# Moving the column sums one chunk on, the spread behind two rounds, and the output weights' split into the q/k/v stage

## The chip, the cores and the metric

The kernel runs on one core of a Trainium2 chip. The metric is the device time of one execution in microseconds. Engines are named as in the profile: PE is TensorE (PEld its weight loads), DVE is VectorE, ACT is ScalarE, POOL is GpSimd and SP is SyncE, which here only issues transfers. Each engine works through its own list of instructions in order and waits on semaphores that other engines and transfers raise.

## The reference, cut to what matters

Two layers run over 2048 rows of width 1024. Layer 0 is sliding-window attention (16 query heads, 4 key and value heads of 64), layer 1 a pooling mixer.

```python
for i in range(DEPTH):                                  # 2 layers
    shift, scale, gate = adaln_params(c, ada_w[i], ada_b[i])   # silu(c) @ w + b, split in three
    h = rms_norm(x, norm_g[i]) * (1.0 + scale) + shift
    # layer 0: q, k, v, g = split(h @ w_in); q, k: norm per head, rotation of 16 columns
    #          branch = (banded_sink_attention(q, k, v) * silu(g)) @ w_out
    # layer 1: branch = (multiscale_pool(v) @ w_group * scale * silu(g)) @ w_out
    x = x + gate * branch
```

Each large product is computed as three products of parts: a float32 operand is split into a high half (rounded to the multiplier's format) and a low half (the rest).

## The kernel before, in words

Four stages follow each other on every engine: q/k/v (to about 371 us), gate (to 572), attend (to about 1000) and pool. Intermediate results go to device memory and come back.

**The q/k/v stage** loops over 16 tiles n of 128 rows. On PE a tile is three projections of 24 products each (`project`, L663: bank 0 and 1 are q, bank 2 is k and v), and between them the transposes of the tile before: `q_round` 0 and 1 after projection 0, rounds 2 and 3 after projection 1 (L679), `k_round` after projection 2 (L686). Round 3 waits until DVE has copied round 1 out (`evict_q`, L529). The normalised input comes in groups s of 256 rows, made two tiles ahead. For it PE sums squares at the end of an odd tile (L641), DVE makes the mean (L446), POOL takes its power -0.5 (`rx`, L301), and in the next even tile PE spreads the result over all partitions (`spread`, L648), which DVE then multiplies in (L452). In the kernel before, `spread` stands between projection 0 and round 0.

ACT squares each bank out of PSUM (L351). For bank 2 it first copies v's high half into the one buffer `vs` (L349), and for that it must wait until the tile before's `vs` has been stored. DVE reduces the squares (L482), POOL takes the power (L306), DVE multiplies (`normalise`, L492). At a tile's end DVE's list reads: `low_q` (L518), the reduction for bank 2, `low_v` (L522), `normalise` of bank 2; at the start of its next tile `low_k` (L534), in even tiles the mean (L446), and the reduction for bank 0.

SP issues all of the stage's transfers, in order, on one queue. Its pass n begins when the keys of tile n-2 have been stored (L256, behind `low_k`). In an even n up to 10 it then issues the store of a group of `ht` (L238, 2 MB) and the load of a group of x (L233, 1 MB), and in every pass tile n-1's `vs` (L251), queries (L254) and keys.

**The gate stage** has 32 chunks q of 24 products (`gate_chunk`, L929) into four PSUM banks. ACT and DVE make the gate from each (L868, L881). Beside this DVE adds 64 pieces of adaLN weights into 8 groups of column sums (`add_ada`, L890 and L892, in the slots that `ada_by(q)` gives), loaded 256 KB at a time by POOL's queue (L827). Once a group is complete, PE adds it over the partitions with four small products (`sum_mods`, L939; eight instructions in the trace), after the very chunk in whose slot the group's last piece is added. In every third slot from 8 on, one eighth of the attention's output weights passes too: SP loads 512 KB into the raw ring (L784), ACT rounds the high half (L857), DVE subtracts the low half (L861), and POOL's queue stores both (L831, 1 MB). `set_mods` (L898 to L901) takes the sums over in the last slot.

Of the kernel before, what the change touches and what calls it, by code (L numbers as in the profile page):

```python
# [40 lines left out]
def build(nc, xt, c_col, positions, ada_w, ada_b, norm_g, attn_w_qkv, attn_w_gate, attn_q_norm, attn_k_norm,  # L41
# [24 lines left out]
    with ExitStack() as top:  # L66
# [6 lines left out]
        def sem(name):  # L73
# [4 lines left out]
                       ht_d, qt_d, kt_d, vs_d, ident, c_silu)  # L78
        ga = gate_stage(nc, sem, dims, weights, qk, attn_w_gate, attn_w_out, ada_w, ada_b, norm_g, ht_d, sg_d, wo_d, c_silu,
# [42 lines left out]
def qkv_stage(nc, sem_of, dims, weights, xt_d, c_col_d, pos_d, ada_w, ada_b, norm_g, w_qkv_d, q_norm, k_norm,  # L122
              ht_d, qt_d, kt_d, vs_d, ident, c_silu):
# [15 lines left out]
    STORED = NS - BANK // TB  # L139
    TWO_PI = 2 * math.pi  # L140
# [50 lines left out]
    qtr_done, ktr_done, act_ev, dve_ev, k_hi, k_lo = (sem(n) for n in ("qtr_done", "ktr_done", "act_ev", "dve_ev", "k_hi", "k_lo"))  # L191
    w_loaded, w_hi, w_lo = weights["loaded"], weights["hi"], weights["lo"]
# [20 lines left out]
    MOD_PARTS = ((0, KC), (KC, KC + KC // 2), (KC + KC // 2, MODC))  # L213
    THIRDS = ((0, 1, 2), (3, 4, 5), (6, 7))
# [15 lines left out]
    def sync(sp, next_load):  # L230
# [26 lines left out]

        sp.dma_start(c_col[:, :], c_col_d).then_inc(c_loaded, 16)
# [63 lines left out]
    def scalar(act, next_hi):  # L322
# [57 lines left out]

        act.wait_ge(c_loaded, 32)
# [54 lines left out]
    def vector(dve, next_lo):  # L436
# [112 lines left out]

        def reduce_angle(quarter, dst):  # L550
# [46 lines left out]
        for n in range(NB + 1):  # L597
# [91 lines left out]
    def tensor(pe):  # L689
# [9 lines left out]
        for n in range(NB):  # L699
# [20 lines left out]
    def last_round(pe, i):  # L720
        q_round(pe, NB - 1, 2 * i)
        q_round(pe, NB - 1, 2 * i + 1)
        if i == 1:
# [3 lines left out]
            "items": ITEMS, "ring": ring_at(ITEMS), "hx_done": hx_done, "proj_done": proj_done, "qtr_done": qtr_done, "mx_done": mx_done, "act_ev": act_ev,  # L727
# [3 lines left out]
def gate_stage(nc, sem_of, dims, weights, qk, w_gate, w_out, ada_w, ada_b, norm_g, ht_d, sg_d, wo_d, c_silu, gate0, mod1):  # L731
# [8 lines left out]
    ITEMS = 2 * KC  # L740
# [7 lines left out]
    def ring(name, n):  # L748
# [4 lines left out]
        ("sg", [P, PER, KC, P], F32), ("wo", [P, 2, KC * P], F32R), ("sums", [P, 2, BANK], F32), ("ada", [P, 4, BANK], F32),  # L753
        ("bias", [P, 2, 3 * KC], F32), ("g_col", [P, KC], F32), ("ones", [P, KC], F32), ("pad", [P, 8 * KB - 8 * KC], F32),
        ("w_first", [P, HEAD, 2, KC * P], F32R), ("raw", [P, RAW, KC * P], F32)])
    sg, wo, sums, ada, bias, g_col, ones, raw = (sb[n] for n in ("sg", "wo", "sums", "ada", "bias", "g_col", "ones", "raw"))
# [5 lines left out]
    ada_loaded, wo_stored, cols_loaded = ring("ada_loaded", 4), sem("wo_stored"), sem("cols_loaded")  # L762
# [13 lines left out]
    def split_of(i, part):  # L776
        if i >= KC:
            return wo[:, part]
        return sb["w_first"][:, i, part] if i < HEAD else sb["w_late"][:, i - HEAD, part]

    def load(sp, i):
        wait(sp, w_lo, ITEM0 + i - RAW + 1)
        src = w_gate[i] if i < KC else w_out[i - KC]
        sp.dma_start(raw[:, (RING0 + i) % RAW], src.rearrange("p k c -> p (k c)")).then_inc(raw_loaded[(RING0 + i) % RAW], 16)  # L784
# [19 lines left out]
    def sync(sp, next_load):  # L804
# [5 lines left out]
        for i in range(RAW + 2, KC + RAW):  # L810
            load(sp, i)
        for q in range(KC, SLOTS):
# [4 lines left out]
            if out_piece(q) is not None and KC + out_piece(q) + RAW < ITEMS:  # L817
                load(sp, KC + out_piece(q) + RAW)
# [4 lines left out]
    def gpsimd(pool):  # L823
# [17 lines left out]
        for q in range(4, SLOTS):  # L841
            for n in range(ada_by(q - 1) + 4, min(ada_by(q) + 4, ADA)):
                load_ada(n)
            if out_piece(q - 1) is not None:
                store_out(out_piece(q - 1))

    def hi(act, i):
# [3 lines left out]
        elif i < KC:  # L851
            act.wait_ge(qk["proj_done"], 3 * NB)
        elif i == KC:
            act.wait_ge(qk["qtr_done"], 4 * NB)
        else:
            act.wait_ge(wo_stored, 16 * (i - KC))
# [6 lines left out]
    def scalar(act):  # L863
# [7 lines left out]
        for q in range(SLOTS):  # L871
# [3 lines left out]
            if out_piece(q) is not None:  # L875
                hi(act, KC + out_piece(q))

    def vector(dve):
# [25 lines left out]
        for q in range(SLOTS):  # L904
# [7 lines left out]
            if out_piece(q) is not None:  # L912
                lo(dve, KC + out_piece(q))

    def tensor(pe, last_round):
# [27 lines left out]
        for q in range(SLOTS):  # L943
# [3 lines left out]
            for j in range(len(JOBS)):  # L947
                if ada_by(q - 1) < KC * (j + 1) <= ada_by(q):
# [4 lines left out]
            "wo_stored": wo_stored, "ada_added": ada_added, "ada_all": ADA, "mod_set": mod_set}  # L953


def attend_stage(nc, sem_of, dims, weights, qk, ga, xt_d, sinks_d, wvt, w_group, qt_d, kt_d, vs_d, sg_d, wo_d, wp_d, x1t_d, ident,
# [23 lines left out]
    def ring(name, n):  # L980
# [33 lines left out]
    fold_hi, fold_lo, wg_hi, wg_lo, fold_done, fold_out = (sem(n) for n in (  # L1014
        "fold_hi", "fold_lo", "wg_hi", "wg_lo", "fold_done", "fold_out"))
# [42 lines left out]
    def load_fold(sp, u):  # L1058
        f, pair = u // PAIRS, u % PAIRS
        if pair == 0:  # L1060
            wait(sp, wg_lo, f - 1)
            sp.dma_start(wg_raw[:, f % 2], w_group[GC * f:GC * (f + 1)].rearrange("c p n -> p c n")).then_inc(wg_loaded[f % 2], 16)
        wait(sp, fold_lo, u - 2)
# [8 lines left out]
    def first_load(sp):  # L1072
# [11 lines left out]
        sp.wait_ge(ga["wo_stored"], 16 * KC)  # L1084
# [84 lines left out]
    def scalar(act, next_hi):  # L1169
# [87 lines left out]
    def vector(dve, next_lo):  # L1257
# [95 lines left out]
    def tensor(pe, spread_first):  # L1353
# [579 lines left out]
```

## Time and profile before

| | before |
|---|---|
| median of 3 runs | 1532.41 us (1531.48 to 1533.28) |
| the profiled execution, its own time | 1531.92 us |
| its span | 1530.2 us |
| PE busy (share of the span) | 1433.7 us (94%) |
| DVE, ACT, POOL busy | 890.7, 537.0, 385.1 us |
| mean granted clock of PE | 0.988 |

The span is the stretch that the trace covers, and the profiled execution's own time is 1.7 us longer. A busy PE can be a slow PE, because its granted clock may fall to half. The granted clock is given as a share of full speed. Where a line of the trace ends in square brackets, they hold the idle time of the engine just before it and what ended it. Times are from the span's start.

### The profile page before, as it was taken

The page shows a single profiled execution, that of the slowest core. Times are in us where ns is not written, and L with a number is a line of the kernel's source. Part 1 is how long each engine was busy: PE and PEld are TensorE (multiplying, and loading weights), DVE is VectorE, ACT ScalarE, POOL GpSimd, SP SyncE. Part 2 cuts the span into 40 slices and gives each one's busy share as a digit, 9 for nine tenths or more (in the row PEclk, how much of TensorE's full clock was granted, in tenths as well). Part 3 has the DMA queues.
Part 4 walks back from the last instruction along what each step waited for, and adds up shares of the span by engine and source line. Part 5 has one row for each costly group of instructions (what it writes and reads, how often), then busy time and mean ns, then how long its engine had stood idle before and what let it go on. Part 6 is the DMA issues. An engine that isn't in the chain of part 4 may idle for free.

```text
span 1530.2 us, 20206 instructions
## 1 busy us (share of the span) xinstructions
PE 1433.7 (94%) x7240; PEld 1209.0 (79%) x7240; DVE 890.7 (58%) x1524; ACT 537.0 (35%) x1270; POOL 385.1 (25%) x551
## 2 busy tenths in 40 slices
PE   1799999999889996789999999899999999999999
PEld 1577777788777886788888888788888888888887
DVE  7766666765544347777777775535456452555522
ACT  2443433333211116775655563322222222222200
POOL 2333333321222213445555554320000000000000
PEclk9999999999999998999999999999999999999999
DMA  8655555434888786766767765841112561112142
GB/s 307 219 180 186 187 188 198 174 134 176 332 314 309 250 325 219 273 233 222 275 237 284 281 234 195 309 124 42 56 42 69 171 199 64 47 51 76 49 151 83
DMA packets 96787, 285.62 MB, mean 187 GB/s; under 512 B 10768, under 2 KB 40496, under 8 KB 87088
## 3 DMA queue, kind: packets, MB, share of 16 engines
q1 hardware_dynamic: 87760, 250.74, 45.8%
q0 software_dynamic: 8928, 33.59, 6.3%
q8 instruction: 58, 0.95, 0.3%
q14 instruction: 41, 0.34, 0.1%
HBM read 196.22 MB, written 88.08 MB: 186 GB/s over the span
## 4 chain that ended last, share of the span: by engine, by line
PE 68%; DMA 10%; DVE 9%; ACT 5%; issue 3%; POOL 2%; SPq 1%; DVEq 0%; ACTq 0%; POOLq 0%
PE po_f_ps L1839 23%; PE po_y_ps L1855 11%; PE at_y_ps L1411 9%; PE qk_proj L663 7%; PE ga_g_ps L929 6%; PE at_o_ps L1395 5%; PE at_s_ps L1367 3%; DMA ga_ada<-in_ada_w 3%; DMA values_split<-qk_late 2%; PE at_tr L1377 2%; DMA po_xn<-x_mid_t 1%; ACT at_pr L1187 1%; POOL qk_rq L306 1%; DMA ga_raw<-in_attn_w_gate 1%; DMA x_mid_t<-at_x 1%
## 5 line engine op out<-in xcount | busy, mean ns | idle before, releaser
L1839 PE MATMUL po_f_ps<-po_ht,po_w 128*128 128x512 f32 x1536 | 348.9, 389 | 0.0
L1839 PEld LDWEIGHTS po_f_ps<-po_ht,po_w 128*128 128x128 f32 x1536 | 288.1, 188 | 60.1 <-DVE po_ht L1701 0.3
L663 PE MATMUL qk_proj<-qk_w_qkv,qk_ht 128*128 128x512 f32 x1152 | 280.5, 399 | 8.1 <-DVE qk_w_qkv L539 4.0
L663 PEld LDWEIGHTS qk_proj<-qk_w_qkv,qk_ht 128*128 128x128 f32 x1152 | 215.2, 191 | 55.1 <-issue 6.1
L1411 PE MATMUL at_y_ps<-at_zt,at_w 128*128 128x512 f32 x768 | 198.9, 400 | 4.5 <-DVE at_x L1300 4.5
L1855 PE MATMUL po_y_ps<-po_zt,po_w 128*128 128x512 f32 x768 | 174.7, 389 | 0.0
L1855 PEld LDWEIGHTS po_y_ps<-po_zt,po_w 128*128 128x128 f32 x768 | 144.1, 188 | 29.9
L1411 PEld LDWEIGHTS at_y_ps<-at_zt,at_w 128*128 128x128 f32 x768 | 138.4, 190 | 30.6 <-issue 6.1
L1688 DVE TENSOR_TENSOR po_w<-po_raw,po_w 128x1024 fp32r<-128x1024 f32 x48 | 58.8, 1225 | 128.1 <-ACT po_w L1622 128.1
L1143 POOL TENSOR_SCALAR_AFFINE_SELECT at_pt<-at_ph 128x512 fp32r<-128x512 f32 x128 | 83.3, 673 | 188.6 <-ACT at_ph L1194 188.6
L306 POOL TENSOR_TENSOR qk_rq<-qk_mq,qk_half 128x8 f32<-128x8 f32 (+1 forms) x48 | 70.2, 1463 | 181.6 <-DVE qk_mq L485 181.5
L1395 PEld LDWEIGHTS at_o_ps<-at_pt,at_vs 128*128 128x128 f32 x744 | 98.3, 194 | 3.8
L1395 PE MATMUL at_o_ps<-at_pt,at_vs 128*128 128x256 f32 x744 | 101.3, 286 | 0.0
L1187 ACT ACTIVATE at_pr<-at_sc,at_neg_max 128x129 f32<-128x129 f32 x256 | 99.6, 393 | 4.0 <-DVE at_neg_max L1265 1.9
L1622 ACT ACTIVATE po_w<-po_raw 128x1024 fp32r<-128x1024 f32 x48 | 50.6, 1053 | 108.4 <-PE po_y_ps L1855 108.4
L1547 POOL DMA_DIRECT2D po_xn<-x_mid_t x32 | 17.4, 544 | 263.3 <-DVE po_ht L1701 257.6
L1769 DVE SCALAR_TENSOR_TENSOR po_x<-po_y_ps,mod,po_x 128x512 f32<-128x512 f32 x32 | 24.0, 751 | 99.7 <-PE po_y_ps L1855 99.7
L1143 POOL TENSOR_SCALAR_AFFINE_SELECT at_pt<-at_pl 128x512 fp32r<-128x512 f32 x128 | 78.5, 636 | 1.2 <-DVE at_pl L1277 0.2
L1367 PE MATMUL at_s_ps<-at_kt,at_qt 128*128 128x256 f32 x512 | 73.4, 287 | 0.0
L929 PE MATMUL ga_g_ps<-ga_x,ga_w_late 128*128 128x512 f32 x288 | 68.8, 399 | 0.0
L868 ACT ACTIVATE ga_sg<-ga_g_ps 128x512 f32<-128x512 f32 x32 | 18.9, 595 | 140.1 <-PE ga_g_ps L929 111.5
L1367 PEld LDWEIGHTS at_s_ps<-at_kt,at_qt 128*128 128x128 f32 x512 | 67.6, 196 | 0.1
(168 smaller groups left out, 1982.9 us busy)
## 6 DMA issues: line engine op xcount, KB each, us to landing
at_w<-out_weight_split SPq DMA_DIRECT2D x32, 1024.0 KB, 6.9
queries_t<-qk_late SPq DMA_DIRECT2D x16, 1024.0 KB, 4.0
ga_ada<-in_ada_w POOLq DMA_DIRECT2D x64, 256.0 KB, 4.8
at_qt<-queries_t SPq DMA_DIRECT2D x16, 1024.0 KB, 8.1
ht_split<-qk_ht SPq DMA_DIRECT2D x6, 2048.0 KB, 9.5
values_split<-qk_late SPq DMA_DIRECT2D x16, 768.0 KB, 6.2
at_vs<-values_split SPq DMA_DIRECT2D x16, 768.0 KB, 5.1
qk_late<-in_ada_w SPq DMA_DIRECT2D x16, 512.0 KB, 6.0
```

The lines of the kernel that those rows point to most:

```text
L306: nc.gpsimd.tensor_tensor(rq[:, heads], mq[:, heads], half[:, heads], ALU.pow).then_inc(rq_done, 1)
L663: last = nc.tensor.matmul(proj[:, b * BANK:(b + 1) * BANK], ht[:, s % 2, m, k, t * P:(t + 1) * P], w_qkv[:, w, k, b * BANK:(b + 1) * BANK] ...
L929: last = nc.tensor.matmul(g_bank(q), split_of(f, w)[:, k * P:(k + 1) * P], h, start=(i == 0), stop=(i == 3 * KC - 1))
L1143: nc.gpsimd.affine_select(out=pt[:, u % 2, kind, :].rearrange("p (h t) -> p h t", h=GROUP), in_=(ph if hi else pl)[:, :].rearrange("p (h t ...
L1187: last = nc.scalar.activation(pr[:, u % 2, h, :], sc[:, g, h, :], ACT.Exp, bias=neg_max[:, u % 2, h:h + 1], accum_out=den[:, u % 2, h:h + 1])
L1367: last = nc.tensor.matmul(s_ps[:, u % 2, h, :, :], qt[:, m % 2, GROUP * g + h, :], kt[:, low:high + 1:high - low, g, part, :], start=(part ...
L1395: last = nc.tensor.matmul(o_ps[:, 0:2 * P], v, moving[:, :, parity, :], start=(i == 0), stop=(i == 6 * len(parts) - 1))
L1411: last = nc.tensor.matmul(y_ps[:, c % 2, :], w[:, c % 3, a, k, :], zt[:, s % 2, b, k, :], start=(k == 0 and (a, b) == PRODUCTS[0]), stop=( ...
L1622: nc.scalar.activation(w[:, i % 2, HI].rearrange("p k c -> p (k c)"), raw[:, (RING0 + i) % RAW].rearrange("p k c -> p (k c)"), ACT.Copy).t ...
L1688: nc.vector.tensor_tensor(w[:, i % 2, LO].rearrange("p k c -> p (k c)"), raw[:, (RING0 + i) % RAW].rearrange("p k c -> p (k c)"), w[:, i % ...
L1839: last = nc.tensor.matmul(f_ps[:, bank(j, h), :], w[:, i % 2, a, k, :], ht[:, h, m, k, :], start=(n == 0), stop=(n == 3 * KC - 1))
L1855: last = nc.tensor.matmul(y_ps[:, h, :], w[:, i % 2, a, k, :], zt[:, h, m, k, :], start=(n == 0), stop=(n == 3 * KC - 1))
```

## The change

1. `sum_mods(j)` runs one chunk later than before.
2. In even tiles of the q/k/v stage `spread` stands behind rounds 0 and 1.
3. The output weights' eight pieces d are split in the q/k/v stage, in tiles 4 to 11, and no longer in the gate stage. The three slots of the raw weight ring, unused there, hold the raw piece and both halves. SP loads piece d at the head of pass 4+d and stores both halves at the head of pass 5+d, ahead of all else in the pass and on its own queue. ACT rounds the high half in the middle of the tile, DVE subtracts the low half at its end.
4. In the attend stage two pairs of semaphores are merged into one each; the waits mean the same. A wait of SP for the stores of the output weights moves from the attend stage to the first gate weights' load.

```diff
@@ qkv_stage
+    FIRST_OUT = 4
+    OUT_RAW, OUT_HI, OUT_LO = 0, 1, 2
@@ sync
+        def load_out(d):
+            sp.wait_ge(w_lo, ITEMS + d)
+            sp.dma_start(raw[:, OUT_RAW, :], w_out[d].rearrange("p k c -> p (k c)")).then_inc(wo_loaded, 16)
+
+        def store_out(d):
+            sp.wait_ge(w_lo, ITEMS + d + 1)
+            sp.dma_start(wo_d[d], raw[:, OUT_HI:OUT_LO + 1, :]).then_inc(wo_stored, 16)
         for n in range(NB + 1):
+            if 0 <= n - FIRST_OUT - 1 < KC:
+                store_out(n - FIRST_OUT - 1)
+            if 0 <= n - FIRST_OUT < KC:
+                load_out(n - FIRST_OUT)
             if n < NB and n % 2 == 0:
                 store_ht(n // 2)
...
@@ scalar
+        def out_high(d):
+            act.wait_ge(wo_loaded, 16 * (d + 1))
+            wait(act, wo_stored, 16 * d)
+            nc.scalar.activation(raw[:, OUT_HI, :].bitcast(F32R), raw[:, OUT_RAW, :], ACT.Copy).then_inc(w_hi, 1)
...
+                if 0 <= n - FIRST_OUT < KC:
+                    out_high(n - FIRST_OUT)
                 split_q(n)
                 square(n, 2)
@@ vector
+        def out_low(d):
+            dve.wait_ge(w_hi, ITEMS + d + 1)
+            nc.vector.tensor_tensor(raw[:, OUT_LO, :].bitcast(F32R), raw[:, OUT_RAW, :], raw[:, OUT_HI, :], ALU.subtract).then_inc(w_lo, 1)
...
                 normalise(n, 2)
+            if 0 <= n - FIRST_OUT < KC:
+                out_low(n - FIRST_OUT)
@@ tensor
-            if n > 0 and n % 2 == 0 and n // 2 + 1 < NS:
-                spread(pe, n // 2 + 1)
             if n > 0:
                 q_round(pe, n - 1, 0)
                 q_round(pe, n - 1, 1)
+            if n > 0 and n % 2 == 0 and n // 2 + 1 < NS:
+                spread(pe, n // 2 + 1)
             project(pe, n, 1)
@@ gate_stage
-    ITEMS = 2 * KC
+    ITEMS = KC
...
-            if out_piece(q) is not None and KC + out_piece(q) + RAW < ITEMS:
-                load(sp, KC + out_piece(q) + RAW)
...
-            if out_piece(q - 1) is not None:
-                store_out(out_piece(q - 1))
...
-            if out_piece(q) is not None:
-                hi(act, KC + out_piece(q))
...
-            if out_piece(q) is not None:
-                lo(dve, KC + out_piece(q))
...
             for j in range(len(JOBS)):
-                if ada_by(q - 1) < KC * (j + 1) <= ada_by(q):
+                if ada_by(q - 2) < KC * (j + 1) <= ada_by(q - 1):
                     sum_mods(j)
```

## Rows read from the trace of the kernel before

**Rows 1.** PE's waits over the whole span: us in total, times, longest.
```profile
PE ga_mod_ps L939 <- DVE ga_sums L892: 8.8, 5, 3.4
PE qk_bc_ps L648 <- POOL qk_rx L301: 8.0, 7, 2.0
```

**Rows 2.** PE in order of time, tiles 8 and 9 (start, us, instruction).
```profile
219.66 0.71 PE L648 MATMUL qk_bc_ps<-ident,qk_rx 128*128 128x128 f32 x4 [0.83 <-POOL qk_rx L301]
220.20 1.04 PE L679 MATMUL qk_tr<-ident,qk_late 128*128 128x128 f32 x8
221.00 5.75 PE L663 MATMUL qk_proj<-qk_w_qkv,qk_ht 128*128 128x512 f32 x24
...
246.48 0.63 PE L679 MATMUL qk_tr<-ident,qk_late 128*128 128x128 f32 x4 [0.71 <-DVE qk_late L529]
```

**Rows 3.** SP's queue in order of time, pass 8 of the q/k/v stage.
```profile
218.79 0.32 SPq L256 DMA_DIRECT2D keys_t<-qk_late  x1
219.16 0.57 SPq L238 DMA_DIRECT2D ht_split<-qk_ht  x1
219.78 3.05 SPq L233 DMA_DIRECT2D qk_x<-in_xt  x1
222.87 4.39 SPq L251 DMA_DIRECT2D values_split<-qk_late  x1
```

**Rows 4.** ACT's waits, 60 to 370 us.
```profile
ACT qk_late L357 <- DVE qk_qkv L513: 57.0, 15, 6.4
...
ACT qk_late L349 <- DMA values_split<-qk_late: 3.3, 3, 1.5
```

**Rows 5.** Chain that ended last, 250 to 290 us: start, us, what.
```profile
258.96 0.32 SPq L256
...
262.91 13.80 DMA values_split<-qk_late
...
280.28 0.60 DVE qk_sq L482
```

**Rows 6.** Stretches: length, busy us of PE, PEld, DVE, ACT, POOL, clock, DMA share, GB/s.
```profile
332.00:334.50 2.50, 2.50 (x15) 2.09 (x14) 1.34 (x3) 1.93 (x4) 0.00 (x0) 1.00 0.89 367
339.20:344.50 5.30, 5.30 (x30) 4.51 (x28) 3.13 (x9) 1.72 (x3) 1.74 (x1) 1.00 0.96 281
439.00:441.00 2.00, 2.00 (x9) 2.00 (x10) 0.49 (x1) 0.00 (x0) 1.09 (x2) 0.50 1.22 516
```

**Rows 7.** PE in order of time, gate stage.
```profile
417.43 7.31 PE L929 MATMUL ga_g_ps<-qk_ht,ga_w_late 128*128 128x512 f32 x24
424.58 11.04 PE L929 MATMUL ga_g_ps<-ga_x,ga_w_first 128*128 128x512 f32 x48
438.98 1.86 PE L939 MATMUL ga_mod_ps<-ga_ones,ga_sums 128*128 128x1 f32 x8 [3.35 <-DVE ga_sums L892]
440.70 13.13 PE L929 MATMUL ga_g_ps<-ga_x,ga_w_late 128*128 128x512 f32 x48
...
489.46 5.60 PE L929 MATMUL ga_g_ps<-ga_y,ga_w_late 128*128 128x512 f32 x24
496.40 1.05 PE L939 MATMUL ga_mod_ps<-ga_ones,ga_sums 128*128 128x1 f32 x8 [1.34 <-DVE ga_sums L892]
```

**Rows 8.** DVE in order of time, gate stage.
```profile
444.97 0.75 DVE L892 SCALAR_TENSOR_TENSOR ga_sums<-ga_ada,c_silu,ga_sums 128x512 f32<-128x512 f32 x1 [5.47 <-DMA ga_ada<-in_ada_w]
```

**Rows 9.** ACT in order of time, 555 to 592 us: one high half.
```profile
560.84 1.05 ACT L857 ACTIVATE ga_wo<-ga_raw 128x1024 fp32r<-128x1024 f32 x1
```

**Rows 10.** DVE, the split's low half: groups by shape, 372 to 572 us.
```profile
L861 DVE TENSOR_TENSOR ga_wo<-ga_raw,ga_wo 128x1024 fp32r<-128x1024 f32 x8 | 9.8, 1225 | 5.1 <-ACT ga_wo L857 5.0
```

**Rows 11.** DVE in order of time, end of tile 8, tile 9.
```profile
238.70 0.68 DVE L534 TENSOR_TENSOR qk_late<-qk_tr,qk_late 128x512 fp32r<-128x512 f32 x1
239.68 0.69 DVE L482 TENSOR_REDUCE qk_sq<-qk_squares 128x8 f32<-128x512 f32 x1 [0.29 <-ACT qk_squares L351]
...
245.66 0.68 DVE L529 CAST qk_late<-qk_tr 128x512 fp32r<-128x512 f32 x1
```

More of the change, by code:

```diff
@@ L752, in gate_stage @@
         ("y", [P, 2, KC, TB], F32R), ("x", [P, 2, KC, TB], F32R), ("w_late", [P, KC - HEAD, 2, KC * P], F32R),
-        ("sg", [P, PER, KC, P], F32), ("wo", [P, 2, KC * P], F32R), ("sums", [P, 2, BANK], F32), ("ada", [P, 4, BANK], F32),
+        ("sg", [P, PER, KC, P], F32), ("pad0", [P, 8 * KB], F32), ("sums", [P, 2, BANK], F32), ("ada", [P, 4, BANK], F32),
         ("bias", [P, 2, 3 * KC], F32), ("g_col", [P, KC], F32), ("ones", [P, KC], F32), ("pad", [P, 8 * KB - 8 * KC], F32),
         ("w_first", [P, HEAD, 2, KC * P], F32R), ("raw", [P, RAW, KC * P], F32)])
-    sg, wo, sums, ada, bias, g_col, ones, raw = (sb[n] for n in ("sg", "wo", "sums", "ada", "bias", "g_col", "ones", "raw"))
+    sg, sums, ada, bias, g_col, ones, raw = (sb[n] for n in ("sg", "sums", "ada", "bias", "g_col", "ones", "raw"))
     ht = (sb["x"], sb["y"])
@@ L768, in g_bank @@
         return g_ps[:, (q + 2) % 4, :]
-    def out_piece(q):
-        return (q - KC) // 3 if q >= KC and (q - KC) % 3 == 0 and (q - KC) // 3 < KC else None
     def ada_by(q):
@@ L776, in split_of @@
     def split_of(i, part):
-        if i >= KC:
-            return wo[:, part]
         return sb["w_first"][:, i, part] if i < HEAD else sb["w_late"][:, i - HEAD, part]
     def load(sp, i):
-        wait(sp, w_lo, ITEM0 + i - RAW + 1)
-        src = w_gate[i] if i < KC else w_out[i - KC]
-        sp.dma_start(raw[:, (RING0 + i) % RAW], src.rearrange("p k c -> p (k c)")).then_inc(raw_loaded[(RING0 + i) % RAW], 16)
+        if i == 0:
+            sp.wait_ge(qk["wo_stored"], 16 * KC)
+        sp.wait_ge(w_lo, ITEM0 + max(i - RAW + 1, 0))
+        sp.dma_start(raw[:, (RING0 + i) % RAW], w_gate[i].rearrange("p k c -> p (k c)")).then_inc(raw_loaded[(RING0 + i) % RAW], 16)
     def load_h(sp, j):
@@ L808, in store @@
                          sg[:, :, :, :].rearrange("p n k t -> p n (k t)")).then_inc(sg_stored, 16)
-        for i in range(RAW + 2, KC + RAW):
+        for i in range(RAW + 2, ITEMS):
             load(sp, i)
@@ L850, in hi @@
             act.wait_ge(qk["hx_done"], KC * (NB // 2 - HEAD + i + 1))
-        elif i < KC:
+        else:
             act.wait_ge(qk["proj_done"], 3 * NB)
[L853 to L856, printed above, removed]
         nc.scalar.activation(split_of(i, HI), raw[:, (RING0 + i) % RAW], ACT.Copy).then_inc(w_hi, 1)
@@ L1013, in attend_stage, with wg_split, wv_split @@
     fold_loaded, wg_loaded, fold_stored = ring("fold_loaded", 3), ring("wg_loaded", 2), ring("fold_stored", 2)
-    fold_hi, fold_lo, wg_hi, wg_lo, fold_done, fold_out = (sem(n) for n in (
-        "fold_hi", "fold_lo", "wg_hi", "wg_lo", "fold_done", "fold_out"))
+    fold_hi, fold_lo, fold_done, fold_out = (sem(n) for n in ("fold_hi", "fold_lo", "fold_done", "fold_out"))
+    def wg_split(f):
+        return f * (PAIRS + 1) + 1
+    def wv_split(u):
+        return wg_split(u // PAIRS) + u % PAIRS + 1
     LAST = UNITS + BEHIND
@@ L1060, in load_fold @@
         if pair == 0:
-            wait(sp, wg_lo, f - 1)
+            if f >= 2:
+                sp.wait_ge(fold_lo, wg_split(f - 2))
             sp.dma_start(wg_raw[:, f % 2], w_group[GC * f:GC * (f + 1)].rearrange("c p n -> p c n")).then_inc(wg_loaded[f % 2], 16)
-        wait(sp, fold_lo, u - 2)
+        if u >= 3:
+            sp.wait_ge(fold_lo, wv_split(u - 3))
         sp.dma_start(wv_raw[:, u % 3], wvt[GC * f:GC * (f + 1)][:, :, pair * ROWS:(pair + 1) * ROWS].rearrange("c p n -> p c n")).then_inc(fold_loaded[u % 3], 16)
@@ L1083, in first_load @@
             load_fold(sp, u)
-        sp.wait_ge(ga["wo_stored"], 16 * KC)
         load_sg(sp, 0)
@@ L1219, in fold_high @@
                 wait(act, fold_done, PAIRS * (f - 1))
-                nc.scalar.activation(wg[:, f % 2, HI], wg_raw[:, f % 2], ACT.Copy).then_inc(wg_hi, 1)
+                nc.scalar.activation(wg[:, f % 2, HI], wg_raw[:, f % 2], ACT.Copy).then_inc(fold_hi, 1)
             act.wait_ge(fold_loaded[u % 3], 16 * (u // 3 + 1))
@@ L1419, in fold @@
             if h == 0:
-                pe.wait_ge(wg_lo, f + 1)
-                pe.wait_ge(fold_lo, u + 1)
+                pe.wait_ge(fold_lo, wv_split(u))
                 wait(pe, fold_out, u - 1)
```

24 lines of the change are left out of this document (11 added, 13 removed).

## The prediction

> **What bounds the kernel now.** I began with PE's waits, because PE is busy 94% of the span. Two of them are what the change touches [rows 1]: the column sums wait 8.8 us for DVE's adaLN adds in the gate stage, in 5 places, and `spread` waits 8.0 us in 7 places for POOL's power. Next comes PE in order of time: `spread` waits 0.83 us in tile 8, and in tile 9 round 3 waits 0.71 us for DVE's copy [rows 2]. So the q/k/v stage is not PE's alone. The third view is what SP issues: at the head of an even pass the keys, `ht`, x and `vs` follow each other, and the issues of x and `vs` themselves take 3.05 and 4.39 us, so the queue is full [rows 3]. Fourth, ACT's waits say who needs that: the copy into `vs` (L349) waits for the last store of `vs` three times, 3.3 us in all [rows 4]. The chain settles it: in the pair of tiles 10 and 11 it runs from the keys' issue at 258.96 through 13.80 us of the `vs` store, which ends at 276.71, and on to DVE's reduction at 280.28 [rows 5]. The two-tile loop thus has a path beside PE with no slack: SP's queue, then ACT, DVE and POOL in turn, then PE's round 3.
>
> **Part 1, the sums one chunk on.** The five waits are 8.8 us [rows 1]. Two of them were long enough to cost twice. After the 3.35 us wait the granted clock is 0.50, the 1.2 GHz level, from 439 to 441 [rows 6]. The eight sum products then take 1.86 us against 1.05, and the next 48 products 13.13 against 11.04 [rows 7]: 0.81 + 2.09 = 2.9 us. After the first long wait 24 products take 7.31 us against 5.60 [rows 7], 1.7 us more. Waits and slow clock make 8.8 + 4.6 = 13.4 us. The same sums come 5.6 us later, more than the longest wait. But PE without its waits also reaches each place earlier, and a transfer paces some adds: one waited 5.47 us for its piece [rows 8]. I leave 0.7 us unrecovered: -12.7 us. Bounds: -13.4, and -6.7 if half the waits come back. The last sums now come after the last chunk, so `set_mods` runs beside ACT's last gate: nothing.
>
> **Part 2, the spread.** The two rounds take 0.8 us to the next instruction (220.20 to 221.00) [rows 2], and would fill the 0.83 us of waiting: -0.8 us per even tile, if POOL's power is not later. It is later where part 3 puts a low half ahead of the mean on DVE, that is in front of tiles 6, 8, 10 and 12. In tiles 6, 8 and 10 the loop below is longer than PE's path anyway, and in tile 4 too. The gain stays in tiles 2 and 12: -1.6 us. Bounds: 0 and -4.8.
>
> **Part 3 in the gate stage.** Eight high halves of 1.05 us [rows 9], eight low halves of 1.2 us [rows 10], their loads and stores and POOL's issues go. All lie beside PE's chunks, and what they delayed are the adds that the sums await; that gain is inside part 1.
>
> **Part 3 in the q/k/v stage.** The high half stands where ACT waits for the rotation, 57.0 us in 15 tiles, 3.8 us each [rows 4]; 1.05 us [rows 9] fits in, and its piece, at the head of the queue, has landed by then. Cost: nothing; 1.05 us a tile if that cover went.
>
> The low half has no such cover. At the end of an even tile it stands in front of `low_k` and of the reduction which starts the next tile's DVE work. In tile 9 the latter idles 0.29 us [rows 11], in tile 11 DVE comes to it straight [rows 5]. From there to the copy for round 3 (239.68 to 245.66) the list leads to PE's wait [rows 2, 11]. At the end of an odd tile it delays `low_k`, hence the keys' store, hence everything that SP issues in the next pass. Each costs 1.2 us [rows 10].
>
> The transfers weigh more. In passes 6, 8 and 10 SP now puts a 1.05 MB store and a 0.52 MB load in front of `ht`, x and `vs`. In pass 10 `vs` lands at 276.71, 17.75 us after the keys' issue [rows 5], and ACT waits for it. From the rows nearest in kind: one queries' store of 1.05 MB runs at 367 GB/s with the engines busy to a share of 0.89 [rows 6], so 2.9 us, or 2.6 at a full share; weight loads of 0.52 MB pieces run at 281 GB/s [rows 6], 1.9 us a piece. Together 4.5 us. From below, 516 GB/s (the fastest stretch, both directions, two queues) [rows 6] would make it 3.0; nothing, if the transfers overlapped fully. From above: 4.8. I take 4.5, since direction and size are the same.
>
> The Trainium skill, "DMA: Bandwidth & Descriptors", section "Where 436 GB/s comes from", puts the ceiling of the 16 transfer engines at 435 GB/s. By that the two transfers would take an estimated 3.6 us, and the sum below would be some 3 us lower. The weight loads' 281 GB/s lie far under it.
>
> The sum for the stage, by pairs of tiles:
> - pairs 6/7 and 10/11: two low halves and the transfers, 2.4 + 4.5 = 6.9 us each; pair 8/9: 0.3 less for its idle DVE, 6.6.
> - pair 4/5: only a load, 1.9, and two low halves, 2.4, less an assumed 0.9 of slack, for ACT did not wait in this pair (three waits, of which the chain shows the longest in tile 10 [rows 4, 5]): 3.4 us.
> - pair 12/13: a store, but no `ht` and no x: hidden.
>
> That is 23.8 us. PE then waits some 6 us in each of these odd tiles, and by the gate stage's example its clock falls for some 2.9 us of loss each time. PE has idle time to pay from, except after the last: +1.0 us, bounds 0 and 5. With part 2: 23.8 + 1.0 - 1.6 = +23.2 us. What is late then is round 3 in tiles 5, 7, 9 and 11.
>
> Behind the freed waits nothing else changes: `vs` in odd passes has neither `ht` nor x ahead of it, and the attend stage keeps its order; part 4 costs nothing.
>
> **Sum.** +23.2 - 12.7 = +10.5 us on the profiled execution's own 1531.92, 1542.4. The median of the runs lies 0.5 us above that execution. I say 1542.5.
>
> **The rivals.**
>
> *A, the transfers hide (the other side, faster).* If the 16 engines took up the `vs` store beside the new transfers, only the low halves would stay: 8 x 1.2 = 9.6, less 1.2 slack and 1.6 of part 2, +6.8; with -12.7 it is 5.9 us faster, 1526.5. The kernel is faster from the point where the transfers cost under 2 us a pair. For it: 516 GB/s is possible [rows 6]. Against it: the x load and the `vs` store already wait on issue [rows 3] and ACT for the landing [rows 4].
>
> Against it also speaks the Trainium skill, "DMA: Bandwidth & Descriptors", section "Queues, rings and completion order": an engine takes one queue's descriptors in the order of their issue and only alternates between queues. POOL's queue carried the stores before; SP's carries them now, ahead of `vs`.
>
> *B, the gate stage's gain is lost.* If the adds are paced by their transfers and not by PE, the sums wait again one chunk on, and half of part 1 is gone: 23.2 - 6.7 = +16.5, 1549. For it: the 5.47 us [rows 8]. Against: the waits are short beside 5.6 us, and the competing weight transfers leave.
>
> *C, the pairs cost half.* If the new store and load cost about 2.2 us a pair and the slacks are larger, the q/k/v stage loses some 16 us and the kernel 3: 1535.5. For it: three landings caused only 3.3 us of waiting together [rows 4], so `vs` is barely late today.
>
> **How the numbers follow.** The forecast has 0.62, with a range of its own from 1537 to 1548: the transfers' bounds give 1.5 less or 0.3 more in each of three pairs, the clock 1 less or 4 more, the sums 0.7 either way. A has 0.16, B 0.10, C 0.12. The range 1530 to 1550 leaves out A and some of B's upper end. About 0.2%, 3.1 us, is what a measurement of this kernel can tell from no change. Faster than 1529.3: A, 0.16. Between: half of C and the forecast's lower edge, 0.08. Slower than 1535.5: 0.76.
>
> **What would show it.** Right: the sums' waits on PE under 1 us and no half clock between 410 and 450; `vs` stores landing 21 to 23 us after the keys' issue in passes 6, 8, 10; ACT's wait at L349 near 5 us each there; PE waiting about 6 us for DVE at round 3 of tiles 7, 9, 11, and a bit over 3 us in tile 5; the gate stage starting near 394 and lasting near 188 us, not 201. Wrong: `vs` landing within 18 us of the keys, or round 3 not waiting; a wait of ACT for the raw piece; or sums that wait as before.

## The result, and the profile after

The changed kernel takes 1536.0 us in the median of 11 runs (1533.4 to 1537.1), the kernel before 1532.7 us beside it. The ratio is 1.0020 with a 95% interval of 1.0010 to 1.0029: slower, by 3.3 us and not by the forecast 10. The profiled execution takes 1535.99 us, its span 1534.3 us, 4.1 us more than before. One of the eleven runs of the kernel before (2052.6 us) and one run of an experiment below (2896.9 us) were slow runs, and the ratios leave them out.

| stretch (bounds: PE's first gate product, PE's first score product) | before | after | difference | forecast |
|---|---|---|---|---|
| q/k/v stage, to the first gate product | 370.73 | 387.56 | +16.8 | +23.2 |
| gate stage | 201.25 | 188.08 | -13.2 | -12.7 |
| attend and pool | 958.2 | 958.7 | +0.4 | 0 |

PE's waits over the whole span of the changed kernel (us in total, times, longest). L708 is the rounds, L677 `spread`, L938 the gate's products:

```profile
PE qk_tr L708 <- DVE qk_late L552: 14.6, 7, 2.9
PE qk_tr L708 <- ACT qk_late L384: 7.3, 3, 3.0
PE qk_bc_ps L677 <- POOL qk_rx L317: 4.1, 3, 2.0
PE ga_g_ps L938 <- DVE ga_w_late L874: 2.8, 2, 1.8
```

The same view of the kernel before has for the rounds and for the gate's products:

```profile
PE qk_tr L679 <- DVE qk_late L529: 4.9, 7, 1.1
PE ga_g_ps L929 <- DVE ga_w_late L861: 1.6, 2, 1.0
```

The column sums are gone from the list, where they had 8.8 us, and `spread` has half of its 8.0 us [rows 1]. In their place the rounds wait 14.6 + 7.3 = 21.9 us, before 4.9. The gate stage, PE in order of time:

```profile
421.15 16.62 PE L938 MATMUL ga_g_ps<-qk_ht,ga_w_late 128*128 128x512 f32 x72 [1.08 <-DVE ga_w_late L874]
437.60 0.95 PE L948 MATMUL ga_mod_ps<-ga_ones,ga_sums 128*128 128x1 f32 x8
438.41 11.19 PE L938 MATMUL ga_g_ps<-ga_x,ga_w_first 128*128 128x512 f32 x48
```

The eight sum products take 0.95 us with no wait ahead of them, and 48 products 11.19 us: neither the 1.86 us nor the 13.13 us of the half clock [rows 7] comes again.

Now the q/k/v stage. SP's queue in order of time, pass 8 of the changed kernel, and the keys with which pass 9 begins:

```profile
225.73 0.32 SPq L260 DMA_DIRECT2D keys_t<-qk_late  x1
226.10 0.53 SPq L268 DMA_DIRECT2D out_weight_split<-qk_raw  x1
226.67 0.69 SPq L264 DMA_DIRECT2D qk_raw<-in_attn_w_out  x1
227.40 1.21 SPq L242 DMA_DIRECT2D ht_split<-qk_ht  x1
228.65 5.49 SPq L237 DMA_DIRECT2D qk_x<-in_xt  x1
234.18 2.85 SPq L255 DMA_DIRECT2D values_split<-qk_late  x1
...
249.94 0.32 SPq L260 DMA_DIRECT2D keys_t<-qk_late  x1
```

The value store is issued 8.45 us behind the keys; before it was 4.08 [rows 3]. The chain of waits in the stretch from 179 to 212 us (start, us, what) shows what that means, in the pair of tiles before, 6 and 7:

```profile
178.09 1.13 DVE qk_raw L575
179.23 0.61 DVE qk_late L557
179.85 0.32 SPq L260
...
182.77 5.30 SPq L237
...
188.11 12.61 DMA values_split<-qk_late
...
200.83 0.07 ACT qk_late L365
...
203.69 1.13 DVE qk_raw L575
204.83 0.60 DVE qk_late L557
205.43 0.60 DVE qk_sq L505
...
211.39 0.61 DVE qk_late L552
```

Read it downwards: tile 5's low half (L575), `low_k` (L557), the keys' issue, x, the value store's landing at 200.72, ACT's copy of v's next high half, tile 6's low half, the reduction, and the copy for round 3. This is the path that the prediction drew through the two-tile loop [rows 5], with both low halves and the new transfers on it. ACT's waits, 60 to 390 us:

```profile
ACT qk_late L365 <- DMA values_split<-qk_late: 14.2, 4, 5.5
ACT qk_late L365 <- PE qk_proj L692: 3.9, 1, 3.9
```

It was 3.3 us in three waits [rows 4]. The 3.9 us stand in pass 8, where PE's projection ended 0.1 us behind the landing of the value store, so that ACT waited for both. And PE at the end of that path, tile 7, in order of time:

```profile
204.71 0.84 PE L692 MATMUL qk_proj<-qk_w_qkv,qk_ht 128*128 128x512 f32 x3
208.57 0.89 PE L708 MATMUL qk_tr<-ident,qk_late 128*128 128x128 f32 x4 [3.01 <-ACT qk_late L384]
212.13 1.09 PE L708 MATMUL qk_tr<-ident,qk_late 128*128 128x128 f32 x4 [2.67 <-DVE qk_late L552]
```

Round 2 waits 3.01 us and round 3 another 2.67; in tile 9 of before it was 0.71 [rows 2].

The price by tiles is read from the starts of the keys' issues in SP's queue (in us, from the profiled execution of each kernel; the last kernel is an experiment told below):

| from the keys of pass | before | after | after, low half cut to a sixteenth |
|---|---|---|---|
| 4 to 6 | 40.17 | 42.93 | 40.58 |
| 6 to 7, 7 to 8 | 20.93, 19.25 | 25.60, 20.28 | 24.56, 19.28 |
| 8 to 9, 9 to 10 | 20.62, 19.55 | 24.21, 20.28 | 24.38, 19.28 |
| 10 to 11, 11 to 12 | 21.34, 19.18 | 25.65, 20.27 | 24.80, 19.27 |
| 4 to 12 | 161.04 | 179.22 | 172.15 |

The four pairs of tiles cost 18.2 us more: +2.8, +5.7, +4.3 and +5.4. Up to pass 4 the changed kernel is 1.5 us ahead, and behind pass 12 it loses 0.2.

### The profile page after: what moved, and what is told of

Its sections match the earlier page's. It is cut to its first block, busy times and chain, and to the rows that moved or that the text cites. A ratio compares the mean times of both kernels' runs of the same rounds, so it can differ in the third digit from the quotient of the medians.

```text
span 1534.3 us, 20205 instructions
## 1 busy us (share of the span) xinstructions
PE 1432.2 (93%) x7240; PEld 1209.5 (79%) x7240; DVE 890.0 (58%) x1524; ACT 537.4 (35%) x1270; POOL 381.6 (25%) x543
## 4 chain that ended last, share of the span: by engine, by line
PE 73%; DVE 9%; DMA 7%; ACT 5%; issue 3%; SPq 2%; POOL 2%; ACTq 0%; DVEq 0%; POOLq 0%
PE po_f_ps L1853 23%; PE po_y_ps L1869 11%; PE ga_g_ps L938 10%; PE at_y_ps L1426 9%; PE qk_proj L692 7%; PE at_o_ps L1410 5%; PE at_s_ps L1382 3%; DMA values_split<-qk_late 2%; PE at_tr L1392 2%; DMA po_xn<-x_mid_t 2%; ACT at_pr L1202 1%; SPq L237 1%; DMA ga_raw<-in_attn_w_gate 1%; POOL qk_rq L322 1%; DMA qk_raw<-in_attn_w_qkv 1%
## 5 line engine op out<-in xcount | busy, mean ns | idle before, releaser
L1561 POOL DMA_DIRECT2D po_xn<-x_mid_t x32 | 17.4, 545 | 262.3 <-DVE po_ht L1715 260.0
L1392 PE MATMUL at_tr<-ident,at_pr 128*128 128x128 f32 x256 | 41.1, 284 | 27.7 <-DVE at_pr L1286 27.7
L938 PE MATMUL ga_g_ps<-ga_x,ga_w_late 128*128 128x512 f32 x288 | 66.5, 390 | 0.0
```

Source lines behind the costliest of these rows:

```text
L938: last = nc.tensor.matmul(g_bank(q), split_of(f, w)[:, k * P:(k + 1) * P], h, start=(i == 0), stop=(i == 3 * KC - 1))
L1392: last = nc.tensor.transpose(tr[:, h * P:(h + 1) * P], pr[:, u % 2, h, 0:P], ident[:, :])
```

## The experiments

The ratios below are to the kernel before, with 95% intervals; "the four pairs" are the time from the keys of pass 4 to those of pass 12, as in the table.

**Part 1 alone, and parts 1 and 2.** Both on the kernel before.

```diff
-                if ada_by(q - 1) < KC * (j + 1) <= ada_by(q):
+                if ada_by(q - 2) < KC * (j + 1) <= ada_by(q - 1):
```


> The kernel before with the column sums one chunk on and nothing else. If the gate stage's gain comes from PE's waits for the sums (8.8 us) and the slow clock after two of them (4.6 us), and the weights' split in the gate stage is covered, the gate stage falls from 201 to 188 or 189 us and the kernel by 12 to 13 us, to about 1520. If the split's transfers and DVE work are what makes the sums late, part of the waits comes back one chunk on and the gain is 6 to 9 us.

Measured: 1520.6 us, ratio 0.9931 (0.9910 to 0.9952). The gate stage lasts 191.5 us; two waits of the sums are left, 2.8 us together. The one-line edit is worth 12.4 us by itself in the medians; in the traces the kernel is 11.7 us shorter, 9.8 in the gate stage and 1.7 ahead of the first keys, where the edit touches nothing. The time is that of the first theory, but the second is right in part: some waiting came back with the split in the stage.

```diff
@@ the above, and
-            if n > 0 and n % 2 == 0 and n // 2 + 1 < NS:
-                spread(pe, n // 2 + 1)
             if n > 0:
                 q_round(pe, n - 1, 0)
                 q_round(pe, n - 1, 1)
+            if n > 0 and n % 2 == 0 and n // 2 + 1 < NS:
+                spread(pe, n // 2 + 1)
```


> The kernel before with the sums one chunk on and the spread behind the two rounds; the output weights stay in the gate stage. If the q/k/v stage is held by the landing of the value store in tiles 6, 8 and 10, the spread gives only 0.8 us in each of tiles 2 and 12 and a part of it in 4: 2 to 2.5 us more than the sums alone, about 1517.5. If PE's path holds it, six tiles give 0.8 us each: 4.8 us more, about 1515.

Measured: 1519.5 us, ratio 0.9916 (0.9899 to 0.9934). In the traces the gate stage starts 4.1 us earlier than with part 1 alone (364.88 against 369.02), the four pairs give 1.7 of it (159.3 against 161.0). The traced run was the fastest of its four; in the medians only 1.1 us show, under both forecasts, and the two intervals overlap. Parts 1 and 2 are thus worth 12 to 14 us, and part 3 costs what the changed kernel has lost since: 16.5 us. That difference holds part 4 too, which no run tests alone; the attend stage and the pool took 958.2 us before and 958.7 after.

**The low halves nearly away.** In the changed kernel DVE subtracts only 64 of 1024 columns, so that fifteen sixteenths of the output weights' low halves are left out; transfers and waits stay.

```diff
-            nc.vector.tensor_tensor(raw[:, OUT_LO, :].bitcast(F32R), raw[:, OUT_RAW, :], raw[:, OUT_HI, :], ALU.subtract)
+            nc.vector.tensor_tensor(raw[:, OUT_LO, 0:64].bitcast(F32R), raw[:, OUT_RAW, 0:64], raw[:, OUT_HI, 0:64], ALU.subtract)
```


> The changed kernel with the low half cut to 64 of 1024 columns (the rest of the low halves is not computed), all transfers kept. If each low half stands in the two-tile loop twice, a pair of tiles loses 2 x 1.1 us: about 8 us over four pairs, less the slack, 6 to 8 us faster than the changed kernel, about 1529. If the transfers alone hold the loop, under 2 us.

Measured: 1527.7 us, ratio 0.9972 (0.9959 to 0.9985); the four pairs 172.2 us. The tiles tell the two costs apart (third column of the table). Odd tiles last 19.28 us as before: store and load cost nothing there, and each full low half costs the 1.0 us by which the changed kernel lies above. Even tiles still last 3.6, 3.8 and 3.5 us longer than before. (With the full low half the even tiles are 1.0 and 0.9 us longer in two pairs and 0.2 shorter in pair 8/9, of which more below.) DVE in order of time shows what is left of the short operation, 0.13 us from its start to the next start:

```profile
219.97 0.21 DVE L575 TENSOR_TENSOR qk_raw<-qk_raw 128x64 fp32r<-128x64 f32 x1
220.10 0.68 DVE L557 TENSOR_TENSOR qk_late<-qk_tr,qk_late 128x512 fp32r<-128x512 f32 x1
```

So the transfers cost some 3.5 us a pair in this kernel.

**The value store first.** The changed kernel, with the value store issued directly behind the keys, ahead of the new store and load, `ht` and x. It stands twice, the second a repetition.

```diff
         for n in range(NB + 1):
+            if n > 0:
+                store_values(n - 1)      # taken out of store_tile(n - 1)
             if 0 <= n - FIRST_OUT - 1 < KC:
                 store_out(n - FIRST_OUT - 1)
```


> The changed kernel with one move: SP stores the tile's values at the head of its pass, ahead of the output weights, the group and x. If the new transfers cost because the value store stands behind them, ACT's wait for it goes, about 3 us in each of three pairs and 1 in the first, besides what the kernel before waited there; round 3's waits fall to what the low half costs, and the kernel falls by 9 to 12 us, to about 1525. If the low half on DVE alone holds the loop, it falls by under 3 us.

> The kernel with the values stored first once more, for a narrower interval and beside the others: 1516 again, 16 to 17 us under the kernel before; the attend stage should take as long as in the kernel before, so that the first look's 1521.6 was a longer attend stage and not the q/k/v stage.

Measured: 1516.1 us, ratio 0.9904 (0.9881 to 0.9927), and 1518.8 us, 0.9910 (0.9896 to 0.9925). All of the same bytes go through the same queue, and 17 to 20 us of the changed kernel are gone, where 9 to 12 had been expected. (Two rounds of one kernel lie 2.7 us apart here, so medians of different rounds are no finer than that. The first one's traced run, 1521.6 us, has 960.8 us from the attend stage on, the second's 957.5.) ACT no longer waits for the value store, and the four pairs last 164.2 and 164.3 us, not 179.2. PE's waits, the second run:

```profile
PE qk_tr L727 <- DVE qk_late L503: 28.6, 2, 23.4
PE qk_tr L712 <- DVE qk_late L556: 7.3, 7, 1.5
PE qk_bc_ps L681 <- POOL qk_rx L321: 7.3, 6, 2.0
```

The rounds (L712) wait 7.3 us, not 21.9, and `spread` (L681) waits again, 7.3 us: the low half now stands ahead of the mean, as the prediction's part 2 has it, and nothing longer hides that. The same bytes stand in the queue, so most of part 3's cost came with the value store's place behind them.

**Both costs away.** The value store first, and the low half cut to 64 columns as above.

> The changed kernel with the values stored first and the low half cut to 64 columns (the rest of the low halves is not computed). With the values first alone a pair of tiles takes 41.1 us; if the 1.8 us above 39.3 are the two low halves, four pairs give 7 us and it runs at about 1509. If other waits take their place (the spread, the raw piece), 1513 or more.

Measured: 1513.2 us, ratio 0.9874 (0.9862 to 0.9887); four pairs 159.7 us, not the 157.2 that the first forecast needs.

**The value store first without part 3.** Once alone on the kernel before, once with parts 1 and 2.

```diff
         for n in range(NB + 1):
+            if n > 0:
+                store_values(n - 1)
             if n < NB and n % 2 == 0:
                 store_ht(n // 2)
```


> The kernel before with one edit: at the head of each pass of the q/k/v stage the value store is issued directly behind the keys, ahead of ht and x; the output weights stay in the gate stage, sums and spread as before. Theory 1 (the value store's place in SP's queue only matters where something of DVE's or ACT's is added to the loop, since before it is late by little: round 3 waits 0.71 us and ACT for the store 3.3 us in all): -1 to -2 us, 1530.5 to 1531.5; ACT's waits for the value store vanish, spread still waits some 0.8 us in even tiles, so the pairs of tiles stay near 40 us and the five waits for the sums stay. Theory 2 (the value store paces the two-tile loop as a whole, as the chain of before suggests): pairs fall to 39.3 us at once and the time by 4 to 6 us, to about 1527.

> The kernel before with the sums one chunk on, the spread behind the rounds, and the values stored at the head of the pass; the output weights stay in the gate stage. Sums and spread alone ran at 1519.5. If the value store's landing held tiles 6 to 11 there (round 3 waits 1.2, 1.2 and 1.8 us against 0.7 in other odd tiles), it runs 2 us faster, at 1517 to 1517.5, and the gate stage still waits about 2.8 us for one sum. If the store's place does not matter without the new transfers, 1519.5.

Measured: alone 1531.3 us, ratio 0.9988 (0.9978 to 0.9998), the four pairs 160.6 us; with parts 1 and 2 1515.6 us, 0.9892 (0.9874 to 0.9909), four pairs 157.2. Alone the edit is worth 1 us: ACT's 3.3 us of waiting were nearly all covered by PE's own waits for `spread`. With `spread` moved as well, every pair lasts 39.3 us and round 3 waits 0.7 us in each odd tile. Against this kernel the value store first *with* the weights' split in the q/k/v stage has four pairs 7 us longer (164.2): 4.5 us are its low halves (with them cut, 159.7), and what the other 2.5 are, transfers or the short low halves, the runs do not tell.

**The low half in another gap.** The value store first, and the low halves of odd tiles moved into the next even tile, behind the copy of round 1.

```diff
@@ vector, after evict_q of round 1
+                if n % 2 == 0 and 0 <= n - 1 - FIRST_OUT < KC:
+                    out_low(n - 1 - FIRST_OUT)
@@ at the end of a tile
-            if 0 <= n - FIRST_OUT < KC:
+            if 0 <= n - FIRST_OUT < KC and n % 2 == 0:
```


> The changed kernel with the values stored first, and the low halves of the odd tiles moved on DVE into the next tile, behind the copy of round 1, where DVE idles about 3 us in even tiles; SP's store and load, and the group and x behind them, then start some 5 us later in even passes. If the low half at the end of an odd tile delays the next pass, spread and round 3, four of them give 1.1 us each: 4 to 4.5 us faster than values first alone, about 1512. If the later transfers reach the raw piece, x or the queries too late, it gives nothing or loses up to 5 us per pair.

Measured: 1527.5 us, ratio 0.9968 (0.9956 to 0.9980), 9 to 11 us worse than with the low halves at the tiles' ends, where 1512 had been hoped for. SP's queue, pass 8:

```profile
219.04 0.32 SPq L262 DMA_DIRECT2D keys_t<-qk_late  x1
219.41 0.43 SPq L255 DMA_DIRECT2D values_split<-qk_late  x1
226.44 0.32 SPq L270 DMA_DIRECT2D out_weight_split<-qk_raw  x1
```

SP issues nothing for 6.6 us: it waits for the moved low half to store it, and `ht`, x and the queries stand behind that store. ACT's waits then hold the queries' store, for which it waited 0.4 to 0.5 us with the low halves at the tiles' ends (and 4.6 us for raw pieces, which it did not await there):

```profile
ACT qk_late L388 <- DMA queries_t<-qk_late: 8.0, 3, 3.1
```

A wait moved off DVE's list came back on SP's queue.

**The order of the new transfers.** The price of 3.5 us is under the forecast's 4.5, and in the changed kernel `ht` ran faster than before. Here the load goes ahead of the store.

```diff
+            if 0 <= n - FIRST_OUT < KC:
+                load_out(n - FIRST_OUT)
             if 0 <= n - FIRST_OUT - 1 < KC:
                 store_out(n - FIRST_OUT - 1)
-            if 0 <= n - FIRST_OUT < KC:
-                load_out(n - FIRST_OUT)
```


> The changed kernel with one edit: at the head of a pass SP issues the load of the next raw piece first and the store of the two halves second, so that ht stands directly behind a store and no longer behind a load. Nothing is left out. Theory 1 (a store that stands directly behind a load moves faster: ht ran at 387 to 389 GB/s behind the load in passes 4, 6 and 8 of the changed kernel, and at 340 to 348 behind a store in the kernel before and in the one with the value store alone ahead): ht falls back to 340 to 350 GB/s, the value store of an even pass lands 0.3 to 0.8 us later than in the changed kernel, that is 19.8 to 21.5 us behind the keys' issue, the pairs last 0.3 to 0.8 us longer, the kernel 1 to 2 us: 1537 to 1538. Theory 2 (ht runs faster because more is in flight ahead of it, in whatever order): ht stays at 385 or more, landings, pairs and the time stay as in the changed kernel, 1536.

Measured: 1535.2 us, ratio 1.0016 (1.0005 to 1.0026), as the changed kernel; pairs 6/7 and 8/9 0.3 us longer, 10/11 0.1 shorter. Stretches of pass 6 (length; busy us of PE, PEld, DVE, ACT, POOL; clock; DMA share; GB/s), each time from the keys' issue to ACT's copy behind the value store, and 2 us of `ht`. Before:

```profile
178.61:196.05 17.44, 16.57 (x85) 14.01 (x86) 10.38 (x26) 5.28 (x9) 4.08 (x3) 1.00 0.94 312
182.60:184.60 2.00, 2.00 (x11) 1.64 (x10) 0.71 (x2) 0.00 (x0) 0.00 (x0) 1.00 1.05 342
```

The changed kernel:

```profile
179.85:200.83 20.98, 20.11 (x100) 16.87 (x101) 10.48 (x26) 5.63 (x9) 4.07 (x3) 1.00 0.97 334
187.85:189.85 2.00, 2.00 (x10) 1.64 (x9) 1.78 (x5) 1.10 (x3) 1.29 (x1) 1.00 1.09 387
```

With the load ahead of the store:

```profile
179.81:201.12 21.31, 20.44 (x102) 17.15 (x103) 10.49 (x26) 5.64 (x9) 4.08 (x3) 1.00 0.95 330
187.81:189.81 2.00, 2.00 (x10) 1.65 (x9) 1.78 (x5) 1.10 (x3) 1.29 (x1) 1.00 1.09 387
```

With the value store first and no part 3 (only a store ahead of `ht`):

```profile
182.32:184.32 2.00, 2.00 (x14) 1.77 (x13) 0.26 (x1) 0.89 (x2) 0.00 (x0) 1.00 1.04 344
```

`ht` moves at 387 GB/s in either order, so it need not stand directly behind the load: the first theory falls, though the value store does land 0.3 us later. With a store alone ahead it stays at 344. The second theory, that more in flight ahead is what counts, does not hold either: in pass 4 of the changed kernel only the 0.52 MB load stands between the keys and `ht`, less than the value store's 0.79 MB, and `ht` moves at 386; in its pass 2, with no load, at 342.

```profile
102.00:104.00 2.00, 2.00 (x10) 1.69 (x9) 0.00 (x0) 0.00 (x0) 0.00 (x0) 1.00 1.04 342
143.80:145.80 2.00, 2.00 (x14) 1.81 (x13) 1.13 (x3) 1.09 (x2) 0.20 (x1) 1.00 1.08 386
```

So it goes with a weight load among the transfers ahead; what the load does to it stays open.

**A version that beats both: the sums two chunks on.** The kernel with parts 1 and 2 and the value store first still waited 2.62 us for one sum. The last group stays one chunk on. The line that goes is that kernel's.

```diff
-                if ada_by(q - 2) < KC * (j + 1) <= ada_by(q - 1):
+                if (late := 2 if j < len(JOBS) - 1 else 1) and ada_by(q - 1 - late) < KC * (j + 1) <= ada_by(q - late):
```


> The kernel before with the sums two chunks on (the last group one chunk on), the spread behind two rounds, and the value store at the head of each pass; the output weights' split stays in the gate stage. With the sums only one chunk on, one of them still waited 2.62 us and its eight products then ran at half clock (1.86 us against 1.05). Theory 1 (the wait is only a matter of distance): another chunk of 5.6 us covers it, PE waits under 0.5 us for all sums together, the clock stays up: -3 to -5 us against that kernel's 1515.6, about 1511.5. Theory 2 (the adds are paced by their transfers, and whatever PE gains by not waiting it meets again at the next group): a wait of 1 to 3 us comes back at another group or at the gate weights, and the time stays at 1514 to 1516.

Measured: 1509.3 us, ratio 0.9852 (0.9839 to 0.9866), 23 us under the kernel before and 27 under the changed one. From 360 to 552 us one wait of PE is left:

```profile
PE ga_g_ps L933 <- DVE qk_late L533: 2.3, 1, 2.3
```

Its gate stage lasts 188.1 us, with the weights' split in it. That is what the changed kernel has without the split (188.08). Moving the weights out of the gate stage gave it nothing that a second chunk of distance does not give.

## Why the prediction was right in sign and wrong in size

**Part 1 was right.** The gate stage lost 13.2 us against 12.7, and 188 us was the length foretold. None of the sums' waits came back (PE's waits for the gate's own weights rose from 1.6 to 2.8 us). The weights' split, which part 3 took out of the stage, was the other half of the cause: with it in place, one chunk leaves a wait of 2.4 to 2.8 us. Whether its transfers or its work on DVE delay the adds was not told apart. Rival B is out.

**Part 2 was right for this kernel.** In tile 2 and tile 12 the move shows, elsewhere SP's path hides it. Up to pass 4 the kernel is 1.5 us ahead: about 0.8 is what `spread` of tile 2 waits less, and some 0.7 lie at the stage's start, which the change does not touch (the first keys are issued between 95.9 and 98.3 us in the traces of the several kernels). Behind pass 12 two terms come to the measured +0.2. The projection behind tile 11's round 3 ran partly at the 1.2 GHz level and took 7.84 us, where before it took 5.72, so that PE is 1.3 us further behind the keys of pass 12; tile 12, without the wait for `spread`, takes 1.1 less.

```profile
303.28 7.84 PE L692 MATMUL qk_proj<-qk_w_qkv,qk_ht 128*128 128x512 f32 x24
```

What I had wrong is why `spread`'s waits matter in the kernel before: SP's path has almost no slack there, but PE's own path with these waits is as long. The value store first gives 0.5 us in the four pairs when alone, `spread` alone 1.7, both together 3.8.

**Part 3: the mechanism was right, one term mis-sized.** The step that failed is the transfers' 4.5 us a pair: they delayed ACT's copy behind the value store by 3.5, 2.5 and 3.2 us. The chain, ACT's waits of near 5 us (5.5, 3.9 and 5.4) and the free odd passes are as foretold. PE's 6 us at round 3 came as two waits of about half, round 2 for ACT and round 3 for DVE: 3.0 + 2.7 us in tile 7, 1.4 + 2.9 in tile 9, 2.9 + 2.9 in tile 11. The path through the passes 6, 8 and 10, from both traces:

| us | before | after |
|---|---|---|
| keys' issue to the landing of the keys | 2.9, 2.8, 2.8 | 2.7, 2.6, 2.6 |
| keys' issue to the landing of the new load | - | 7.6, 7.6, 7.6 |
| keys' issue to the landing of `ht` | 9.8, 10.2, 9.7 | 13.5, 13.5, 14.0 |
| keys' issue to the landing of the value store | 17.3, 17.0, 17.8 | 20.9, 19.5, 20.7 |
| keys' issue to ACT's copy behind it | 17.4, 17.1, 17.9 | 21.0, 19.6, 21.0 |
| that copy to the next keys' issue | 3.5, 3.5, 3.5 | 4.6, 4.6, 4.6 |

So the landings lie under the 21 to 23 us that I had given, and the three passes cost 9.2 us, not 13.5: 4.3 of the missing 5.6 us in the pairs (23.8 forecast, 18.2 measured). The low halves give 1.1 us behind each copy and 1.0, 0.7 and 1.1 in the odd tiles, 6.3 for the forecast 6.9: 0.6. Pair 4/5 gives another 0.6 (2.8 for 3.4), and the start of the stage 0.7: 4.3 + 0.6 + 0.6 + 0.7 = 6.2, of 23.2 - 16.8 = 6.4. With the low halves cut short the copy came 3.5, 3.6 and 3.3 us later than before; why the value store of pass 8 landed sooner in the changed kernel, the runs do not tell.

Why 4.5 was too much: I took the time that the two transfers need for the time by which they delay what stands behind them. Their own time was not overrated: the load landed 5.0 us behind the keys in every one of the three passes. But the queue caught up behind it. `ht` landed 5.9, 5.9 and 6.4 us behind the load, while before it landed 6.9, 7.4 and 6.9 behind the keys; in pass 6 an estimated 0.7 us of this is the rate of `ht`, 2.1 MB at 387 and not 342 GB/s. In passes 8 and 10 the value store in its turn followed `ht` 0.8 and 1.4 us closer than before; why, stays open. The stretches from the keys' issue to ACT's copy in passes 8 and 10, before:

```profile
218.79:235.92 17.13, 16.30 (x85) 13.74 (x85) 10.07 (x26) 5.28 (x9) 4.07 (x3) 1.00 0.93 313
258.96:276.82 17.86, 17.04 (x88) 14.41 (x88) 10.58 (x26) 5.29 (x10) 4.07 (x3) 1.00 0.92 306
```

After:

```profile
225.73:245.31 19.58, 19.58 (x101) 16.40 (x100) 10.56 (x26) 6.24 (x10) 4.08 (x3) 1.00 0.98 338
270.22:291.25 21.03, 21.03 (x110) 17.70 (x110) 10.56 (x26) 6.24 (x11) 4.08 (x3) 1.00 0.95 335
```

Pass 6 moves 334 GB/s times 20.98 us = 7.0 MB, before 312 times 17.44 = 5.4 MB: 1.57 MB more in 3.5 us, 444 GB/s at the margin; in passes 8 and 10 it is 514 and 498. In the mean the three passes cost 3.1 us, near the lower bound of 3.0, but that bound was luck. Its 516 GB/s [rows 6] counts what started within two microseconds; over the eight around them the rate is 432 GB/s, by which the bound is an estimated 3.6 us:

```profile
436.00:444.00 8.00, 5.03 (x16) 4.35 (x17) 3.06 (x4) 1.49 (x3) 1.09 (x2) 0.63 1.01 432
```

No rate of a stretch, the fast one or the ones of "same direction and size", gives the delay; the catching up has to be counted too.

By the Trainium skill, "DMA: Bandwidth & Descriptors", section "Where 436 GB/s comes from", whose ceiling for the 16 ports into SBUF is 435 GB/s, the estimate was 3.6 us a pair; the 3.5 us of pass 6 agree with that, and passes 8 and 10 cost less. The stretches as a whole stay under the ceiling, at 334 to 338 GB/s, and so do the eight microseconds at 432. The same section has a limit of some 358 GB/s for transfers between device memory and SBUF; the 387 GB/s of `ht`, a store of that kind, stand against it, and the measurement decides.

**The rivals.** A (the transfers hide) is refuted: they cost 2.5 to 3.5 us a pair. C named the time that came, 1535.5, and in part the cause: the transfers cost 3.1 us a pair in the mean, between its 2.2 and the forecast's 4.5, and what else is missing lies in the low halves, pair 4/5 and the start. A slip of the prediction's sum is small beside this: 1542.4 and 0.5 make 1542.9 and not 1542.5. The stages' measured differences, 16.8 - 13.2 + 0.4, make the 4.1 us of the span.

**What I did not see** is how much hangs on the order in the queue: I named the value store as the path and priced what stands ahead of it, but did not ask what it would give to put the store itself ahead.

## What to carry to other kernels

When the chain runs through the landing of one transfer, look at its place in the queue first: here the kernel with the same transfers in another order took 17 to 20 us less. A transfer that joins a filled queue delays what stands behind it by less than its own time, if the queue can catch up: here 2.5 to 3.5 us for 5.0. And a wait that one chunk of distance does not quite cover may be cured by a second chunk, before any work is moved to another stage where it meets another chain.

## What the runs showed of the hardware

In these kernels `ht`'s 2 MB store moved at 340 to 348 GB/s behind stores alone, and at about 387 where a 0.52 MB weight load was among the transfers ahead of it, in either order and by itself. I had not expected the load to pay back part of its own time. By the Trainium skill, "DMA: Bandwidth & Descriptors", section "Two DMAs through the same engine are not ordered", the read side and the write side of a transfer engine are separate queues, so that transfers of one queue can overlap; no run here shows that this is the cause.

And PE's short waits cost its clock here too: with 5.7 us of waiting in tile 7 the mean granted clock from 179 to 225 us is 0.93, while that stretch before has 1.00. It is 0.50, the 1.2 GHz level, from 208.8 to 215.6, behind the 3.01 us wait of round 2. In tile 5, where round 3 alone waited 2.94 us, the clock stayed at 1.00 (160 to 180 us).

```profile
179.00:225.00 46.00, 39.23 (x186) 32.14 (x185) 29.66 (x68) 17.56 (x36) 14.54 (x14) 0.93 0.67 240
```

Before, over the same tiles:

```profile
178.60:224.00 45.40, 42.99 (x218) 35.82 (x218) 30.66 (x75) 17.58 (x37) 16.99 (x16) 1.00 0.59 207
```
